# Four unread 128x128 transposes at ten places ahead of weight products, and two of TensorE's loops written out

## What is computed

```python
def first_block(x, w_in_even, w_out_even, ...):
    for l in range(DEPTH):                    # 2 layers
        m = even_mixer(x, ...) if l % 2 == 0 else odd_mixer(x, ...)
        x = layer_norm(ALPHA * x + m, ...)
        f = conv_ffn(x, w_up[l], conv_w[l], conv_b[l], w_down[l])
        x = layer_norm(ALPHA * x + f, ...)
    return x
```

## Time and profile before

| | |
|---|---|
| median of 3 runs | 2685.77 us (2677.89 to 2689.56) |
| profiled execution: span from the first to the last instruction | 2679.4 us |
| TensorE busy (matmuls) | 2603.0 us, 97% |
| DVE, ACT busy | 1483.2 us (55%), 1241.3 us (46%) |
| granted TensorE clock | 0.8 of full speed in one of 40 slices, 0.9 or more in the rest |

### The profile page before, as it was taken

How to read it: one execution, slowest core, us unless ns; L and a number is a source line. 1 busy time by engine, 2 the same in 40 slices (tenths; PEclk the granted TensorE clock), 3 DMA queues, 4 the chain that set the end, 5 groups by cost and what they waited for, 6 DMA issues and landing times.

```text
span 2679.4 us, 51068 instructions
## 1 busy us (share of the span) xinstructions
PE 2603.0 (97%) x20904; PEld 2408.2 (90%) x20904; DVE 1483.2 (55%) x2490; ACT 1241.3 (46%) x2037; POOL 114.9 (4%) x178
## 2 busy tenths in 40 slices
PE   8999999999999999999999999989999999999998
PEld 8985999999997599999989877779966998999998
DVE  5235666543424776664467989862476354544433
ACT  4237344432425844442364887852475243444422
POOL 0000000000000000000001223300000000000000
PEclk9999999999998999999999999999999999999999
DMA  6420122223321023233344665632211231323232
GB/s 198 122 71 1 64 95 94 94 96 106 113 95 63 9 72 102 96 99 118 101 159 147 212 196 186 189 126 97 93 55 56 95 126 41 102 94 97 99 103 71
DMA packets 76142, 278.34 MB, mean 104 GB/s; under 512 B 9802, under 2 KB 12010, under 8 KB 75488
## 3 DMA queue, kind: packets, MB, share of 16 engines
q1 hardware_dynamic: 62112, 217.42, 24.3%
q0 software_dynamic: 13888, 58.88, 7.6%
HBM read 267.03 MB, written 9.24 MB: 103 GB/s over the span
## 4 chain that ended last, share of the span: by engine, by line
PE 77%; DVE 12%; ACT 6%; DMA 3%; issue 2%; POOL 0%; DVEq 0%; SPq 0%; ACTq 0%
PE acc L348 64%; PE acc L379 3%; DMA w_raw<-in_stream 2%; DVE big L1851 1%; PE ps L379 1%; DVE res_tmp L2150 1%; DVE big L2479 1%; ACT res_tmp L2120 1%; DVE w_lo L329 1%; PE acc L1351 1%; DVE big L1503 1%; ACT w_hi L323 1%; DVE res_tmp L2144 1%; PE ps L463 1%; PE ps L769 1%
## 5 line engine op out<-in xcount | busy, mean ns | idle before, releaser
L348 PE MATMUL acc<-x_split,w_hi 128*128 128x256 f32 x7936 | 1242.4, 279 | 7.7 <-ACT big L661 2.9
L348 PEld LDWEIGHTS acc<-x_split,w_hi 128*128 128x128 f32 x7936 | 1061.5, 189 | 10.6 <-issue 7.2
L348 PE MATMUL acc<-x_split,w_lo 128*128 128x256 f32 x3968 | 780.7, 278 | 0.0
L329 DVE TENSOR_TENSOR w_lo<-w_raw,w_hi 128x1024 fp32r<-128x1024 f32 x405 | 494.5, 1222 | 482.1 <-ACT w_hi L323 482.1
L323 ACT ACTIVATE w_hi<-w_raw 128x1024 fp32r<-128x1024 f32 x405 | 427.0, 1055 | 588.5 <-PE acc L348 525.7
L348 PEld LDWEIGHTS acc<-x_split,w_lo 128*128 128x128 f32 x3968 | 602.1, 189 | 0.0
L348 PE MATMUL acc<-big_r,w_hi 128*128 128x256 f32 x3376 | 528.4, 279 | 0.6 <-DVE big_r L2532 0.6
L348 PEld LDWEIGHTS acc<-big_r,w_hi 128*128 128x128 f32 x3376 | 451.7, 189 | 1.5 <-DVE big_r L2532 0.8
L348 PE MATMUL acc<-big_r,w_lo 128*128 128x256 f32 x1688 | 332.8, 279 | 0.0
L348 PEld LDWEIGHTS acc<-big_r,w_lo 128*128 128x128 f32 x1688 | 256.2, 188 | 0.0
L1066 ACT ACTIVATE res_tmp<-acc,par 128x512 f32<-128x512 f32 x84 | 64.8, 772 | 142.5 <-PE acc L348 138.0
(11 more groups left out here) (356 smaller groups left out, 2739.9 us busy)
## 6 DMA issues: line engine op xcount, KB each, us to landing
w_raw<-in_stream SPq DMA_DIRECT2D x405, 512.0 KB, 3.5
res_tmp<-scratch_rows POOLq DMA_DIRECT2D x96, 320.0 KB, 5.2
big<-scratch_rows POOLq DMA_DIRECT2D x32, 320.0 KB, 6.1
scratch_bias<-res_tmp POOLq DMA_DIRECT2D x1, 2560.0 KB, 56.0
res_tmp<-in_x SPq DMA_DIRECT2D x2, 1024.0 KB, 6.8
res_tmp<-scratch_bias POOLq DMA_DIRECT2D x8, 256.0 KB, 4.0
scratch_x<-res_tmp POOLq DMA_DIRECT2D x1, 2048.0 KB, 7.8
scratch_kv<-big POOLq DMA_DIRECT2D x1, 2048.0 KB, 8.3
```

What stands on the lines that cost most here:

```text
L329: dve.tensor_tensor(w_lo[:, u.slot], w_raw[:, u.slot], w_hi[:, u.slot].bitcast(F32), ALU.subtract).then_inc(lo_done, 1)
L348: mm = pe.matmul(a[:, h], w, AR[:, x + k, h], start=(k == 0 and w is wh and x == hi and h.start == 0), stop=(k == total - 1 and w is wl), ...
```

## The change

A helper `settle` writes four transposes of the identity matrix into a `ps` bank; nobody reads them. It is called at ten places on TensorE: once in `even_in` behind `bias_pe`, in `head_pe` ahead of the first tile behind the four halved ones (so in `up0`, `odd_in` and `up1`), at the start of `even_out`, in `down1` behind `mem_sum_pe`, at the start of `gated_pe` (so in `br_ssd` and `br_attn`), in `xattn_pe` behind the last `values`, and in `ffn_pe` behind `rms_pe`. In `head_pe` TensorE waits for the bank and the weights first, in the other places the transposes stand ahead of those waits. The loops of `even_in_pe` and `head_pe` become Python loops, so that 24, 40, 20 and 40 tiles are written out where a loop held four each. No other engine's program changes.

```diff
+        def settle(pe, bank):
+            for c in range(CH):
+                pe.transpose(ps[:, bank, c * P:(c + 1) * P], ident, ident)
...
-            with pe.Fori(1, dict((a, b) for a, b, _ in STAGES)[stage] // 4) as i:
+            for i in range(1, dict((a, b) for a, b, _ in STAGES)[stage] // 4):
                 for j in range(4):
-                    product_tile(pe, Units(UB[stage] + j, i, 4), tile_of(stage, j, i), hi, lo)
+                    u, t = Units(UB[stage] + j, i, 4), tile_of(stage, j, i)
+                    if i == 1 and j == 0:
+                        pe.wait_ge(acc_free[t.bank], t.in_bank + 1)
+                        pe.wait_ge(lo_done, u.count + 1)
+                        settle(pe, 4)
+                    product_tile(pe, u, t, hi, lo)
...
             bias_pe(pe)
-            with pe.Fori(1, 7) as i:
+            settle(pe, 3)
+            for i in range(1, 7):
                 body(i)
...
+            if stage == "even_out":
+                settle(pe, 3)
             for n in range(stage == "odd_out", KD - TAIL[stage]):
...
                 if stage == "down1" and j == 4:
                     mem_sum_pe(pe)
+                    settle(pe, 1)
...
         def gated_pe(pe, stage, hi, lo, blocks, ready):
             per = 1 + len(blocks)
+            settle(pe, 3 if stage == "br_ssd" else 0)
...
             for step in range(XD * MC):
                 values(X_H - 1, step)
+            settle(pe, 0)
             product_part(pe, *t1, (4, 5), outs)
...
                     if ready is not None and j == 0:
                         rms_pe(pe, 2)
+                        settle(pe, 3)
```

## The result

The changed kernel takes 2693.03 us (median of 22 runs, 2681.14 to 2713.31), the kernel before on the same chip 2688.32 us (22 runs, 2666.61 to 2704.84). The ratio of the comparison is 1.0039 with a 95% interval of 1.0021 to 1.0056: slower by 0.4%, some 10 us, where 0.7% less had been forecast. The two medians lie only 4.7 us apart, so the direction is sure and the size less so. That is within the 0.5% named as the bound, on its slower side, inside the range and near its upper end. Two executions in the comparisons further down took some 4325 us at a granted clock of 0.56, and the ratios leave them out.

A forecast was written before the change was run, and what follows sets the result against it. TensorE, busy 97% of the span, was taken as the bound. 2679.4 - 19.7 (long-pace stretches) + 4.0 (transposes) - 0.7 (loops) gave 2663.0 us of span; 2666 us was forecast, range 2657 to 2694.

The forecast's parts named there:

- The two paces: Stretches holding only weight products on TensorE run at 113.3 or 117.8 ns a product, a difference of 4.46 ns, 3.8%.
- Do transposes settle the pace?: At the calls, four transposes bring the short pace to long-pace stretches behind them, saving 19.7 us; chance 0.54.
- `down1` (1.9 us): The 418 products behind `mem_sum_pe` in `down1` go from long to short pace, saving 1.9 us.
- `br_attn` (3.4): The 763 products in `br_attn` go from long to short pace, saving 3.4 us.
- `xout` (1.7): The 370 products at the end of `xout` go from long to short pace, saving 1.7 us.
- `up0`/`down0` (12.7): The 2837 products of `up0`/`down0` go from long to short pace, saving 12.7 us, the largest term.
- Transposes: Each call of four transposes costs TensorE 0.44 us; nine calls lie on the path, adding 4.0 us, 4.6 at most.
- Loops written out: Without loop entries in `up0` and `up1`, 0.33 us each, 0.7 us is saved; fetching straight code costs 0.
- The 6.3 us: Profiled span lies 6.3 us under the median: either time around the span, or the profile drew better paces.
- No influence: Rival: paces behind the calls are drawn as before, so the change takes 2674 to 2694 us; chance 0.30.
- The slower one: Rival: transposes fed straight from a busy array bring the long pace; 7822 products lose 34.9 us, span 2718; chance 0.13.
- two thresholds: Slower rival: 740 net products turning long (3.3 us) decide against the change; some 3700 make it over 0.5% slower.

The follow-up runs named there:

- picked kernel: Kernel before with loops written out, four transposes only ahead of the end of `down1`, `br_ssd` and `br_attn`, three ahead of the end of `xout`: 2674.87 us, ratio 0.9960.
- later comparison: The changed kernel run again, unedited, on one chip beside the kernel before and two other variants: 2691.88 us against 2681.25, ratio 1.0047.

## Why the prediction was wrong

**The two paces** were read rightly: in every profile the stretches full of products ran at 113.3 or 117.8 ns a product at full granted clock, and the time followed the count of products at each.

**The step that failed** is "Do transposes settle the pace?". I took the transposes of `ssd` for what brings the short pace, since twelve of fifteen pairs had it, and set four long stretches down as a gain of 19.7 us "if these stretches go over and the others stay as they are". Both halves failed. The patterns behind 100 tiles show that transposes move a state on and don't set it; so a stretch with the short pace can lose it by the same four instructions. The evidence from one profile was weak as well: behind the 16 transposes of `mem_pe`, counted as long, the changed kernel's profile has the short pace (263 products from 1268.9 us). Of the terms, `down1` (1.9 us) and `br_attn` (3.4) came as forecast, in eight of eight profiles with four transposes there. `xout` (1.7) stayed long in eight of eight. `up0`/`down0` (12.7) has either pace with the transposes (s, L, L, s in the four profiles of the changed kernel and of the one without the feed-forward's call) and without (L, s, L in before, with the loops written out alone, and in the picked kernel): nothing to win there but by luck of one execution, and the profile of before had drawn the long one, at the wait for a bank two tiles behind the call. And the feed-forward, short before, is long in seven of seven profiles with four transposes ahead of it and short in four of four without any transposes.

**The small terms** held in size. Transposes: 0.44 and 0.46 us a call against 0.44, where the 273 ns of the earlier trace rows for each would have made 1.09. Loops written out: ratio 0.9988 (0.9961 to 1.0015), which includes the forecast 0.7 us but is too wide to show it. The reason given for them was wrong, though: the 0.33 us of the earlier trace rows is no loop's entry but the wait for a bank, 0.27 us of it is still there in `up0` with the loops alone written out, and it is gone in the changed kernel, where the transposes hold the third tile up for longer than that. `even_in` stayed hidden under its wait.

**The sum as it should have been:** feed-forward +13.7, transposes +4.0, `br_attn` -3.4, `down1` -1.9, the waits of the earlier trace rows -0.7, the rest drawn as before: +11.7 us. Measured were 10.5 us (5.6 to 15.1, from the ratio by 2688.32; 4.7 between the medians) and in the later comparison 12.6 us (5.4 to 19.8).

**The 6.3 us** between the span and the median were mostly another draw of paces: the changed kernel's profiled execution took 2703.2 us with a span of 2701.3, so 1.9 us lie around it and 4.4 are left for the draw.

**The rivals.** "No influence" gave 2674 to 2694 and so the right size, but not the reason, as some places do answer. The slower one, that transposes fed straight from a busy array bring the long pace, is what happens in the feed-forward and the end of `xout`, and isn't what happens in `down1`, `br_ssd` (short in seven of eight) and `br_attn`, which are fed in the same way. As a rule it is wrong too; with eight transposes these five came out the other way round. Its two thresholds count the cost of the transposes with the wrong sign: with 3.3 us of cost the change loses already when no product changes its pace, and 0.5% (13.4 us) is passed from some 2300 products on, not 3700.

**Open** is what the state is. It is moved by the number of transposes and is not set by a wait of TensorE for itself. Besides the distance of the products' starts it shows in their weight loads. These are the changed kernel's, at the short pace (500 to 520 us) and at the long one (2400 to 2420 us), with the least, median and longest duration in ns:

```profile
L348 PEld LDWEIGHTS acc<-x_split,w_hi x118: 187/188/188, 499.9 to 519.7; 128*128 128x128 f32 x118
L348 PEld LDWEIGHTS acc<-x_split,w_hi x115: 187/188/192, 2399.9 to 2419.9; 128*128 128x128 f32 x115
```

At the short pace all loads take 187 or 188 ns; at the long one every third load takes 192, and the others stay as they are. That the state is how the weight loads stand to the matmuls fits this, but it is my guess and wasn't shown: the loads may follow the pace and not make it. Why `up0`, `odd_in` and `up1` draw their pace, while most later places are fixed, isn't settled either; nor was any number but four tried often enough to call a place fixed by it.

## What to carry to other kernels

Before you cure a pace that differs between like stretches, take a second profile of the same kernel: what changes sides from execution to execution is no target, and a gain that is worked out from one draw is half luck. When a disturbance seems to go with the better pace, put it ahead of a hundred tiles in one kernel and read the pattern, which tells a reset from a step. Follow the stretch back to where its pace began, which need not be where the code changes; and count the stretches that already have the better pace as things to lose. Choose places by trial and leave the others alone: one call of four transposes, 0.45 us by itself, cost 14 to 17 us here.

## What the runs showed of the hardware

- Identical products (128x128 weights, 128x256 activations, a weight load ahead of each) have two paces at full granted clock, 113.3 and 117.8 ns, and hold one for up to 3078 products.
- Four transposes ahead of every tile of 48 products give a strict pattern of three (long, short, short) over 100 tiles; one gave long in 100 of 100, three short in 100 of 100 from the state found there. One and three mixed show at least three states.
- A wait of TensorE for its own last product ahead of a tile doesn't reset the pace; 57 of 100 tiles came out long.
- At the long pace every third weight load takes 192 ns; all others, and all at the short pace, take 187 or 188 (changed kernel, feed-forward and `up0`).
- TensorE enters a loop (`up0`, kernel before) without a step: 113 ns from the last product ahead of it to the first one in it.
- 108 tiles of straight code in place of a loop are fetched without a gap that shows: 2.41 MB in 147 packets, 0.4% of the DMA engines.
